# A triangular inverse by doubling: the level mask goes from VectorE, behind the matrix product, to GpSimd, ahead of it

## The reference

```python
m = where(strict, einsum('bhnid,bhnjd->bhnij', k_beta, k) * decay, 0.0)   # strictly lower, 64 x 64
a = m + eye(CHUNK)
sol = triangular_solve(a, rhs, left_side=True, lower=True, unit_diagonal=True)
```

## Time and profile before

| | |
|---|---|
| time, median of 3 runs | 1934.11 us (1933.26 to 1935.99) |
| time of the profiled execution | 1935.99 us |
| its span, first to last instruction | 1934.2 us |
| PE busy / DVE / ACT / POOL | 98% / 64% / 50% / 16% of the span |
| stretch of the delta rule in L = 0, 84 to 160 us: DVE busy | 58.10 of 76.00 us |

### The profile page before, as it was taken

The page is one execution under the profiler, slowest core; times in us unless marked ns, Lnnn a source line. Parts: engine busy times, 40 slices in busy tenths (PEclk is TensorE's granted clock), DMA queues, the critical chain, the costliest instruction groups (busy, mean ns, idle before and its releaser), DMA issues.

```text
span 1934.2 us, 35101 instructions
## 1 busy us (share of the span) xinstructions
PE 1887.0 (98%) x14820; PEld 1800.6 (93%) x14820; DVE 1238.2 (64%) x1667; ACT 958.4 (50%) x1375; POOL 311.4 (16%) x174
## 2 busy tenths in 40 slices
PE   7999999999999999999999999999999999999998
PEld 7989998998889999999988999999999999999997
DVE  6884577665579545867657775577646684567743
ACT  5533365544563344654445445655534444656632
POOL 1050121000014102200001352310000353220000
PEclk9999999999999999999999999999999999999999
DMA  5443344656344323545665553345555763345652
GB/s 209 158 138 108 121 161 140 215 196 205 134 142 159 115 99 127 201 164 186 196 206 176 178 190 121 132 153 198 188 186 172 219 191 123 131 161 176 197 196 99
DMA packets 91580, 317.50 MB, mean 164 GB/s; under 512 B 11552, under 2 KB 12704, under 8 KB 91040
## 3 DMA queue, kind: packets, MB, share of 16 engines
q1 hardware_dynamic: 91424, 315.26, 48.7%
HBM read 304.99 MB, written 1.05 MB: 158 GB/s over the span
## 4 chain that ended last, share of the span: by engine, by line
PE 83%; DVE 12%; ACT 4%; issue 1%; DMA 0%; SPq 0%; ACTq 0%; DVEq 0%
PE bank L1863 81%; DVE wlo L1056 4%; DVE area L1056 3%; DVE area L1062 2%; ACT area L618 1%; ACT whi L624 1%; PE bank L2302 1%; PE bank L2042 1%; DVE xT L1062 0%; DMA raw<-in_weights 0%; DVE hl L1062 0%; DVE area L1527 0%; ACT hh L618 0%; DVE area L1525 0%; PE bank L2320 0%
## 5 line engine op out<-in xcount | busy, mean ns | idle before, releaser
L1056 DVE TENSOR_TENSOR wlo<-raw,whi 128x1024 fp32r<-128x1024 f32 x512 | 657.0, 1296 | 427.6 <-ACT whi L624 427.2
L1863 PE MATMUL bank<-hh,whi 128*128 128x256 f32 x2928 | 834.0, 285 | 26.4 <-DVE wlo L1056 18.7
L1863 PE MATMUL bank<-hl,whi 128*128 128x256 f32 x2928 | 817.6, 279 | 0.0
L1863 PE MATMUL bank<-hh,wlo 128*128 128x256 f32 x2928 | 817.4, 279 | 0.0
L624 ACT CAST whi<-raw 128x1024 fp32r<-128x1024 f32 x572 | 588.2, 1046 | 398.5 <-PE bank L1863 368.5
L1863 PEld LDWEIGHTS bank<-hh,whi 128*128 128x128 f32 x2928 | 556.9, 190 | 41.8 <-issue 15.1
L1863 PEld LDWEIGHTS bank<-hl,whi 128*128 128x128 f32 x2928 | 556.0, 190 | 1.5 <-issue 1.4
L1863 PEld LDWEIGHTS bank<-hh,wlo 128*128 128x128 f32 x2928 | 555.7, 190 | 0.0
L1655 POOL TENSOR_TENSOR area<-area 128x512 f32<-128x512 f32 (+4 forms) x90 | 138.3, 1544 | 929.8 <-ACT area L618 675.9
L1655 POOL TENSOR_TENSOR wlo<-raw,whi 128x1024 fp32r<-128x1024 f32 x60 | 151.5, 2526 | 332.1 <-ACT whi L624 331.7
L1863 PE MATMUL bank<-area 128*128 128x128 f32 (+5 forms) x1544 | 200.3, 289 | 4.1 <-DVE area L1056 3.3
(11 more groups left out here) (123 smaller groups left out, 1883.6 us busy)
## 6 DMA issues: line engine op xcount, KB each, us to landing
raw<-in_weights SPq DMA_DIRECT2D x572, 512.0 KB, 3.7
area<-area SPq DMA_DIRECT2D x96, 64.0 KB, 3.7
area<-area SPq DMA_DIRECT2D x16, 128.0 KB, 3.8
cst<-in_const SPq DMA_DIRECT2D x1, 1188.0 KB, 10.1
cst<-in_const SPq DMA_DIRECT2D x1, 1024.5 KB, 5.6
xT<-in_x SPq DMA_DIRECT2D x4, 256.0 KB, 5.8
out<-xT SPq DMA_DIRECT2D x1, 1024.0 KB, 3.8
area<-in_lev SPq DMA_DIRECT2D x2, 384.0 KB, 7.7
```

The lines of the kernel that those rows point to most:

```text
L1056: return v.tensor_tensor(dst, x, y, op)
L1863: return e.matmul(ps, x, y, start=start, stop=stop, skip_group_check=skip)
```

## The change

The mask is applied to the left factor before the product instead of to the product. `MT` is multiplied by the transposed mask of level s on POOL, one operation of 128 x 1024, into a new buffer `LT` (slot 14); PE multiplies by `LT`; ACT copies the product to `T0`. DVE no longer takes part between the two products. The waits move with it: the product of level 1 now waits for `L` of POOL and for `Y` of level 0, where it waited for `X` of level 0; POOL's `Aq` times `EG` no longer waits for `Y`; POOL makes the mask of level s + 1 after the product `LX` of level s is done.

```diff
@@ scalar: delta
                 for s in range(1, 6):
+                    for j in range(2):
+                        a.wait_ge(*e_dn.at("LX", L, s, j))
+                        a.copy(pair(T0, j), bank[j][:, :]).then_inc(*a_dn.up("T0", L, s, j))
                     if s > 1:
@@ vector: delta
                 for s in range(1, 6):
-                    for j in range(2):
-                        v.wait_ge(*e_dn.at("LX", L, s, j))
-                        tt(quarter(pair(T0, j)), quarter(bank[j]), wide(lev(s), 1, 4), OP.mult).then_inc(*v_dn.up("T0", L, s, j))
                     yield 1
@@ gpsimd: delta
+            def levels_of(L, s):
+                tt(v3(LT, 128), v3(MT, 128), wide(lev(s, True), 1, 8), OP.mult).then_inc(*g_dn.up("L", L, s))
...
                 yield 1
                 yield 2
+                g.wait_ge(*a_dn.at("MT", L, 1))
+                levels_of(L, 1)
                 yield 1
                 g.wait_ge(*e_dn.at("KQ", L, 1))
-
-                g.wait_ge(*v_dn.at("Y", L, 0))
                 tt(Aq[:, :], Aq[:, :], EG[:, :], OP.mult).then_inc(*g_dn.up("q", L))
                 yield 1
                 for s in range(1, 6):
+                    if s < 5:
+                        g.wait_ge(*e_dn.at("LX", L, s, 1))
+                        levels_of(L, s + 1)
                     yield 1
                     yield 1
@@ tensor: delta
                 for s in range(1, 6):
+                    e.wait_ge(*g_dn.at("L", L, s))
                     if s == 1:
-                        e.wait_ge(*a_dn.at("MT", L, 1))
-                        e.wait_ge(*v_dn.at("X", L, 0))
+                        e.wait_ge(*v_dn.at("Y", L, 0))
                     else:
                         e.wait_ge(*v_dn.at("X", L, s - 1, 1))
-
-                    fresh2(0, lambda j: v_dn.at("T0", L, s, j))
-                    blocks(("LX", L, s), MT, X, 0)
+                    fresh2(0, lambda j: a_dn.at("T0", L, s, j))
+                    blocks(("LX", L, s), LT, X, 0)
...
                     yield 1
-                    e.wait_ge(*v_dn.at("T0", L, s, 1))
-                    e.wait_ge(*(a_dn.at("Y", L, s, 1) if s > 1 else v_dn.at("Y", L, 0)))
+                    e.wait_ge(*(a_dn.at("Y", L, s, 1) if s > 1 else a_dn.at("T0", L, s, 1)))
```

More of the change, by code:

```diff
@@ L362, in program @@
         T0, EG, DT, M, MT, AT = (slot(6 + i) for i in range(6))
-        X, Y = slot(12), slot(13)
+        X, Y, LT = slot(12), slot(13), slot(14)
         SV = slot(15)
```

## The result

The changed kernel takes 1944.62 us (median of 6 runs, 1940.01 to 1947.66), the kernel before 1933.08 (6 runs, 1928.06 to 1935.99). The ratio is 1.0061, 95% interval 1.0043 to 1.0080: 0.6% slower. The forecast was 1944.5. The profiled execution took 1948.02, of which the span is 1946.2.

What follows compares the result with a forecast made beforehand. PE, busy 98%, bounds the kernel, and only its waits in the doubling can move. 4.95 - 1.82 + 0.75 + 1.3 gives 5.2 us a layer, 10.4 in two; against the median of 1934.11 that is 1944.5, range 1934.5 to 1949.5.

Steps and rivals of the forecast that it cites:

- The bound and the place: Whole kernel: PE's unchanged work bounds it; only PE's waits in the doubling can move, 5.0 us in two layers.
- POOL and DVE exclude each other: Operations of POOL and DVE with two SBUF inputs: one runs to its end while the other waits, 2.25 us per mask.
- the three DVE operations: DVE's row before Y's end, layer 0: the split at 97.93, X's second and Y's first, each meeting a POOL operation.
- The rival in which POOL's work hides: Doubling: POOL's operations do not hold DVE's; 1.5 to 2.5 us gained a layer, 1929.1 to 1931.1; chance 0.10.
- Who goes first: When both queue, POOL goes in between DVE's neighbouring operations; `LX` of level 1 then starts 4.95 us late.
- DVE keeps its place: Rival before `LX` 1: only mask 1 goes in, POOL's others wait; 0 to +4 us in all, 1934 to 1938; chance 0.14.
- The wait of the first `LX` on Y: Level 1: waiting for Y instead of X costs nothing alone, as Y ended at 103.94 and `LX` started at 104.30.
- The old wait at `XLX` 1: Level 1: PE's wait of 1.82 us for `T0` from DVE disappears, leaving PE 3.13 late.
- The ACT copies: All five levels: ten copies out of PSUM, 1.08 us a pair, hidden behind PE's chunk; without that cover 1.1 a level.
- What is late next: Level 2: `LX` waits 0.75 us more for X of level 1, then `XT` is 5.2 late through the key banks.
- Masks 2 to 5: Mask 2 delays X of level 1; masks 3 to 5 use slack and cost PE nothing.
- the pile-up: Rival: X of level 1 and the key banks each meet one more POOL operation; 7 to 9.5 a layer, 1948 to 1953; chance 0.10.

Runs made afterwards that it cites:

- q_waits_y: Changed kernel with one old wait put back: POOL's `Aq` times `EG` waits for Y of level 0 again; 1937.7 us, ratio 1.0028 to the kernel before.
- no_masks: Changed kernel without POOL's five masks, `LX` taken from `MT` itself, so the inverse is not computed; 1938.11 us, ratio 1.0020 to the kernel before.
- before_pool_late: Kernel before, with POOL's `Aq` times `EG` and pooling held back until X of level 1; 1935.55 us, ratio 1.0004.
- mask1_dve_late: Kernel before with the new scheme in level 1 alone, its mask made by DVE, and POOL's pooling waiting for X of level 1; 1929.89 us, ratio 0.9974.
- before_q_early: Kernel before with one part of the change alone: POOL's `Aq` times `EG` no longer waits for Y of level 0; 1943.77 us, ratio 1.0055.
- lx_waits_x: Changed kernel, but the first `LX` waits for X of level 0 as before, and `XLX` 1 waits for Y; 1948.93 us, ratio 1.0078 to the kernel before.
- fill_wait: Changed kernel with 20 spare products on PE ahead of each layer's first `LX`, filling its wait; 1943.15 us, ratio 1.0044 to the kernel before.
- rest_gpsimd: mask1_dve_late with the change's scheme in levels 2 to 5 as well, masks on POOL and `T0` copies on ACT; 1945.88 us, ratio 1.0035 to the kernel before.

## Why the prediction was right

**The bound and the place.** Right. PE's work is unchanged, and in layer 0 the pieces shift by 5.27 up to `LX` 3 and by nothing from there to the end of level 5. In layer 1 they shift by 4.38 (27.44 us from `KQ` to `LX` 3 before, 31.82 after). Together 9.65 of the forecast 10.4. The other 2.4 of the 12.0 that the profiled span grew lie outside the doubling: `KQ` of layer 0 starts 0.5 sooner, the stretch from `LX` 3 of layer 0 to `KQ` of layer 1 takes 5.0 more, and what follows `LX` 3 of layer 1 takes 2.2 less. In the 5.0 us lies the recurrence of layer 0, with the half clock for 13.6 us against 3.4 in the kernel before; the half clock there lies in another place in nearly every trace, and nothing here shows that the change is its cause. So it is in part luck that the forecast of 1944.5 and the 1944.62 agree so closely: by the medians of 6 runs the time grew by 11.5, not 10.4, and the kernel before was 1.0 faster than in the three runs that the forecast started from. One wait was overlooked: before `LX` 3 PE loses 0.2 in the kernel before (4.73 from `XLX` 2 where 4.55 is the undelayed time). It is gone in the change, which is most of the step from 5.53 to 5.27.

**POOL and DVE exclude each other.** Right, in both directions and to the size: 2.16 (3.38 - 1.22), 2.07 and 0.83 more for the three DVE operations, beside POOL operations that hold for 2.38, 2.25 and 0.89 (the forecast had 2.25, 2.25 and 1.03). Taking POOL's operations away made records normal again and PE's starts earlier in four runs (q_waits_y, no_masks, before_pool_late, mask1_dve_late); the total time shows it in the first two, against the change. Letting `Aq` times `EG` in early in the kernel before, with the copy behind it, and nothing else, gave a loss of the same kind (before_q_early). The Trainium skill, GPSIMD Engine Reference, section Key points, has contention for DVE instructions with two SBUF inputs; the traces agree. Beyond that sentence they show that it is whole operations that wait, and that POOL's copy with one input holds them too (2.05 instead of 1.22, beside a copy that takes 1.03 undisturbed). The rival in which POOL's work hides is refuted.

**Who goes first.** Right: POOL goes in between DVE's neighbours, before X's second and before Y's. The rival "DVE keeps its place" would have had `LX` 1 only 1.85 late.

**The wait of the first `LX` on Y.** Right that alone it costs nothing and that the lateness of Y does; lx_waits_x shows that PE's being let past it is worth nothing either.

**The old wait at `XLX` 1.** Right: the 1.82 is gone, in the change and in every run with ScalarE's copies. The ACT copies (0.59 each) were hidden as said.

**What is late next.** Here the step failed as it stood, although the sum held. The forecast was that `LX` 2 waits 0.75 for X and `XT` 2 another 1.3 for the key banks. In the changed kernel `LX` 2 waits for nothing and `XT` 2 as long as before (0.52; in layer 1 0.85). In their place stands the granted clock, which the prediction did not mention: half of full speed for 6.8 us from within the idle 4.65 on, with 2.5 us lost at `XLX` 1 (5.61 against the 3.12 of fill_wait). In layer 1 it is 3.4 us from within an idle 4.40 on, and 1.2 us (4.30 against 3.06). Since it delays PE and not DVE, DVE catches up meanwhile. fill_wait separates the two: without the fall the two waits are there, in the forecast's size. That the two have the same price is a coincidence of this kernel.

**Masks 2 to 5 and the pile-up.** No wait for POOL in the change, as forecast; no pile-up.

## What to carry to other kernels

An engine with 36% idle time is not free where its operations stand in an unbroken row ahead of a wait of TensorE; moving work from VectorE to GpSimd cost VectorE the whole length of GpSimd's operation where both took their inputs from SBUF, here 2.2 us for an operation that VectorE does in 1.2. The same holds for waits: one taken away on an idle engine can let its work slip into another engine's critical row, so give background work a wait that sends it to a stretch where the other engine works out of PSUM or has slack. And when waits of TensorE grow, look at the granted clock behind them before adding up the next waits; here it fell with waits of 3 to 5 us, and in q_waits_y with 0.89 and 1.90 close together.

## What was not expected of the hardware

**The clock behind a wait.** Within idle times of 4.65 us (the change), 4.92 (lx_waits_x) and 4.19 (before_q_early) the granted clock fell, to 0.50 for 6.8 us in layer 0, into the work behind them; in the kernel before, with 1.65, it stayed at 1.00. It also fell with shorter waits, if not always: in rest_gpsimd at the end of an idle 3.11 in layer 0, to 0.50 for 3.4 us, but not with 3.21 in layer 1; in q_waits_y behind 0.89 and 1.90 with one product between them, for 3.4 us in both layers. In fill_wait, with 0.69 and 1.51 in the same places, it stayed at 1.00. In the recurrence of both layers half-clock stretches of 3.4 or 6.8 us lie in another place in nearly every trace, from 6.8 to 20 us in all.

**Two paces at the same clock.** In stages of projections alone, TensorE runs at one of two paces in an execution, with the granted clock at 1.00 and no idle time. The stretches of 1770 to 1900 us, first of the kernel before, then of before_pool_late:

```profile
1770.00:1900.00 130.00, 130.00 (x1150) 130.00 (x1149) 75.60 (x74) 65.47 (x75) 0.00 (x0) 1.00 0.59 197
```

```profile
1770.00:1900.00 130.00, 130.00 (x1106) 130.00 (x1106) 74.62 (x74) 63.66 (x73) 0.00 (x0) 1.00 0.59 190
```

1150 matmuls against 1106 in the same 130 us, 113.0 and 117.5 ns each, with nothing of the kernel different there. The last 1400 matmuls of the program take 161.4 us in the first and 167.4 in the second, 6.0 more, which is more than most effects studied here, and the slower pace falls now on one stage, now on another. With the half clocks it can account for a large part of the 10 us and more by which the times of one kernel scatter; no two traces of one kernel are at hand to show it. Its cause stays open.
